# Cross attention of a streaming encoder layer: the samples' matmuls in column groups, splits cut by head and in quarters

## What is computed

```python
qx = (rms_norm(h, g_pre_x) @ wq_x).reshape(bsz, l, MEM_HEADS, MEM_HEAD_DIM)
s = jnp.einsum('bqhd,bmhd->bhqm', qx.astype(f32), mem_k.astype(f32)) / math.sqrt(MEM_HEAD_DIM)
p = jax.nn.softmax(s, axis=-1)
ox = jnp.einsum('bhqm,bmhd->bqhd', p, mem_v.astype(f32)).reshape(bsz, l, D_MODEL).astype(dtype)
h = h + rms_norm(ox @ wo_x, g_post_x)
```

## Time and profile before

| | before |
|---|---|
| median of 3 runs | 2054.76 us |
| profiled execution | 2048.69 us, span of its instructions 2046.7 us |
| PE busy | 1916.4 us, 94% of the span |
| DVE, ACT, POOL busy | 937.4, 540.9, 422.4 us |
| mean granted PE clock | 0.966 of 2.4 GHz |
| chain that ended last | PE 80%, DVE 11%, ACT 4%, issue 4% |

### The profile page before, as it was taken

How to read it: one execution, slowest core, us unless ns; L and a number is a source line. 1 busy time by engine, 2 the same in 40 slices (tenths; PEclk the granted TensorE clock), 3 DMA queues, 4 the chain that set the end, 5 groups by cost and what they waited for, 6 DMA issues and landing times.

```text
span 2046.7 us, 28884 instructions
## 1 busy us (share of the span) xinstructions
PE 1916.4 (94%) x12014; PEld 1850.7 (90%) x12014; DVE 937.4 (46%) x1600; ACT 540.9 (26%) x1144; POOL 422.4 (21%) x203
## 2 busy tenths in 40 slices
PE   7999989998777898989989899999999999999996
PEld 7998979998666798988889899999999999999995
DVE  6852276675775428324342752332232232333245
ACT  6432312224663325103232541001001001001023
POOL 0000001131000132310023233143153153153130
PEclk9999999998899899989989999999999999999998
DMA  5243122222105311122311221011011011011032
GB/s 192 73 146 130 57 90 84 62 83 86 32 11 173 110 42 41 62 101 106 129 57 42 94 72 49 24 52 52 21 52 52 21 52 52 21 62 42 21 113 93
DMA packets 61950, 146.22 MB, mean 71 GB/s; under 512 B 4352, under 2 KB 34432, under 8 KB 60288
## 3 DMA queue, kind: packets, MB, share of 16 engines
q1 hardware_dynamic: 33952, 103.53, 14.8%
q10 hardware_dynamic: 27872, 40.88, 5.8%
HBM read 120.95 MB, written 23.44 MB: 71 GB/s over the span
## 4 chain that ended last, share of the span: by engine, by line
PE 80%; DVE 11%; ACT 4%; issue 4%; DMA 1%; SPq 1%; ACTq 0%; DVEq 0%
PE bank L200 23%; PE bank L203 22%; PE bank L204 22%; PE bank L1088 2%; PE bank L1099 1%; PE bank L1058 1%; PE bank L887 1%; DVE NL L281 1%; PE bank L966 1%; PE bank L914 1%; DVE hid_l L2312 1%; DMA w_raw<-in_wall 1%; DVE at_sm L2043 1%; PE bank L267 1%; PE bank L736 1%
## 5 line engine op out<-in xcount | busy, mean ns | idle before, releaser
L203 PE MATMUL bank<-NL,w_hi 128*128 128x384 f32 x1800 | 609.0, 338 | 0.0
L200 PE MATMUL bank<-NH,w_hi 128*128 128x384 f32 x1608 | 548.7, 341 | 9.0 <-DVE NL L340 6.6
L204 PE MATMUL bank<-NH,w_lo 128*128 128x384 f32 x1608 | 543.8, 338 | 0.0
L581 POOL TENSOR_TENSOR w_hi<-w_raw,one 128x1024 fp32r<-128x1024 f32 x82 | 163.7, 1996 | 1006.8 <-PE bank L200 881.2
L203 PEld LDWEIGHTS bank<-NL,w_hi 128*128 128x128 f32 x1800 | 340.9, 189 | 2.3 <-issue 0.9
L200 PEld LDWEIGHTS bank<-NH,w_hi 128*128 128x128 f32 x1608 | 304.7, 189 | 11.4 <-DVE NL L340 6.7
L204 PEld LDWEIGHTS bank<-NH,w_lo 128*128 128x128 f32 x1608 | 304.4, 189 | 0.0
L583 POOL TENSOR_TENSOR w_lo<-w_raw,w_hi 128x1024 fp32r<-128x1024 f32 x90 | 232.0, 2579 | 104.9 <-ACT w_hi L332 98.4
L2295 DVE TENSOR_TENSOR ACC<-ACC,bank 128x384 f32<-128x384 f32 x240 | 132.2, 553 | 124.1 <-PE bank L204 124.0
L200 PE MATMUL bank<-hid_h,w_hi 128*128 128x384 f32 x528 | 181.8, 344 | 5.5 <-DVE ACC L2295 4.7
L203 PE MATMUL bank<-hid_l,w_hi 128*128 128x384 f32 x528 | 177.8, 337 | 0.0
(11 more groups left out here) (345 smaller groups left out, 2831.5 us busy)
## 6 DMA issues: line engine op xcount, KB each, us to landing
w_raw<-in_wall SPq DMA_DIRECT2D x130, 512.0 KB, 3.3
cK<-in_cmk SPq DMA_DIRECT2D x8, 1024.0 KB, 7.0
cV<-in_cmv SPq DMA_DIRECT2D x8, 1024.0 KB, 4.9
H<-in_xT SPq DMA_DIRECT2D x5, 1536.0 KB, 12.5
scratch_h<-H ACTq DMA_DIRECT2D x3, 1536.0 KB, 5.9
Hback<-scratch_h ACTq DMA_DIRECT2D x3, 1536.0 KB, 11.8
out_y<-Hback ACTq DMA_DIRECT2D x6, 768.0 KB, 3.6
Kb<-in_kc SPq DMA_DIRECT2D x6, 512.0 KB, 9.3
```

Of the source, the lines that this page charges most:

```text
L200: m = mm(out, ah, bh, start=(i == 0), stop=False)
L203: mm(out, ah, bl, start=False, stop=False)
L204: m = mm(out, al, bh, start=False, stop=(i == n - 1))
L581: pool.tensor_tensor(whi[s][:], raw[s % 2][:], bc(one[:, 0:1], [P, WI]), ALU.mult).then_inc(w_hi, 1)
```

## The change

1. **Column groups.** y_scores(b) becomes, for each half e of the head dimension, four matmuls with 32 columns of weights (16 queries and 16 zeros, xQz), each head writing its own 32 PSUM partitions. Scores then stand on 128 partitions instead of 64, and the vector and activation steps on them too. y_values(b) turns round: the probabilities are the weights (32 columns), the cached values move (256 columns), each head again on its own 32 partitions. Its output isn't transposed, so ACT copies it (`y_ocopy` to sO), PE transposes it (`y_otrans`, one round later) and DVE copies it to QX.
2. **First tile and keys by head.** QXh gets a place of its own, tile 0 gets its own QXl0, and ACT and DVE go head by head: query part, key part. The scores of a head wait for that head alone. QXl0 lies in the place of cK1, so SP waits for the scores of tile 0 before cK1.
3. **Quarters.** The first chunk's split behind either attention is made in four pieces of two k, high and low, and the first unit waits for each piece where it needs it.
4. The loads of q and k of a tile become two steps with a semaphore each; q's goes out a head earlier.
5. Some semaphores of the samples' self attention are used again (b_S, b_nb, b_exp, b_p) with counts that go on.

```diff
-                         [("xQbd", [P, 2, H * QB], F32), ("mkh", [P, KT, MEM], F32R), ("xE0", [P, H, MEM], F32), ("xE1", [P, H, MEM], F32),
-                          ("xPT", [P, 2 * H * P], F32), ("cK1", [P, KT, MEM], F32)],
+                         [("xQz", [P, 2, KT, 32], F32), ("mkh", [P, KT, MEM], F32R), ("xE0", [P, H, MEM], F32), ("xE1", [P, H, MEM], F32),
+                          ("xPT", [P, 2 * H * P], F32), ("QXh", [P, KT, P], F32R), ("cK1", [P, KT, MEM], F32)],
+                         [("under_cK1", [P, 8 * MEM + 2 * 256 + 3 * 1024 + KT * P], F32), ("QXl0", [P, KT, P], F32R)],
...
-                          ("cV0", [P, 2, D], F32), ("sE0", [64, MEM], F32), ("sE1", [64, MEM], F32),
-                          ("sPT", [P, 2, 64], F32)]))
+                          ("cV0", [P, 2, D], F32), ("sE0", [P, MEM], F32), ("sE1", [P, MEM], F32),
+                          ("sPT", [P, 2, P], F32), ("sO", [P, MEM], F32)]))
...
+                if split is not None and i % 2 == 0:
+                    nc.tensor.wait_ge(n_lo, split + i // 2 + 1)
...
+                if b == 1:
+                    sp.wait_ge(x_S, 1)
                 if b >= 2:
-                    sp.wait_ge(y_S, b - 1)
...
+                pe.wait_ge(ld_qk[w], 16 * max(2, t + 1))
...
+                if q in (4, 8):
+                    pe.wait_ge(n_lo, SPLIT_Y + q // 4 + 4)
+                lin_unit(pe, I_WO, 0, q, YH, NL, split=None if q else SPLIT_Y)
...
-            pe.wait_ge(mk_l, 1)
 
             def x_scores(t):
-                pe.wait_ge(x_ql, t + 1)
                 if t:
+                    pe.wait_ge(x_ql, t)
                     pe.wait_ge(x_exp, H * t)
                 for h in range(H):
+                    if t == 0:
+                        pe.wait_ge(mk_l, 2 * h + 2)
                     m = three(B[h // 2][:, MEM * (h % 2):MEM * (h % 2) + MEM],
-                              [(g("QXh")[:, k, :], g("QXl")[:, k, :], g("mkh")[:, k, :], g("mkl")[:, k, :])
+                              [(g("QXh")[:, k, :], g("QXl" if t else "QXl0")[:, k, :], g("mkh")[:, k, :], g("mkl")[:, k, :])
...
-                for k in range(KT):
-                    m = mm(B[6][0:64, 0:MEM], g("xQbd")[:, b % 2, 64 * k:64 * k + 64], g(f"cK{b % 2}")[:, k, :], start=(k == 0),
-                           stop=(k == KT - 1))
-                m.then_inc(y_S, 1)
+                    pe.wait_ge(b_exp, DB + b)
+                for e in range(2):
+                    for h in range(H):
+                        m = mm(B[6][rows_of(h), 0:MEM], g("xQz")[:, b % 2, 2 * h + e, :], g(f"cK{b % 2}")[:, 2 * h + e, :],
+                               start=(e == 0), stop=(e == 1))
+                m.then_inc(b_S, 1)
...
             def y_trans(b):
-                pe.wait_ge(y_p, b + 1)
+                pe.wait_ge(b_p, DB + b + 1)
                 if b:
                     pe.wait_ge(ys_o, b)
                 for k in range(2):
-                    m = nc.tensor.transpose(B[7][:, 64 * k:64 * k + 64], g(f"sE{b % 2}")[:, tok(k)], ident[0:64, 0:64])
...
             def y_values(b):
                 pe.wait_ge(y_Te, b + 1)
                 pe.wait_ge(ld_cv[b % 2], 16 * (b // 2 + 1))
-                for h in range(H):
-                    for e in range(2):
-                        o = B[7][:, P + DS * (2 * h + e):P + DS * (2 * h + e) + DS]
-                        for k in range(2):
-                            m = mm(o, g(f"cV{b % 2}")[:, k, tok(2 * h + e)], g("sPT")[:, k, DS * h:DS * h + DS],
-                                   start=(k == 0), stop=(k == 1))
+                for k in range(2):
+                    for h in range(H):
+                        m = mm(B[7][rows_of(h), MEM:2 * MEM], g("sPT")[:, k, rows_of(h)],
+                               g(f"cV{b % 2}")[:, k, MEM * h:MEM * h + MEM], start=(k == 0), stop=(k == 1))
                 m.then_inc(y_pv, 1)
+
+            def y_otrans(b):
+                pe.wait_ge(y_c, b + 1)
+                for e in range(2):
+                    m = nc.tensor.transpose(B[7][:, tok(e)], g("sO")[:, tok(e)], ident)
+                m.then_inc(y_ot, 1)
 
...
+                if i:
+                    y_otrans(i - 1)
                 x_trans(i)
                 if i + 1 < DB:
                     y_scores(i + 1)
                 y_trans(i)
                 x_values(i)
                 y_values(i)
+            y_otrans(DB - 1)
 
...
+            def load_qk(t, w):
                 if t > 2:
-                    act.wait_ge(a_tr, 2 * t)
+                    act.wait_ge(a_tr, 2 * t + w - 1)
                 dst = g("qkr" if t > 1 else f"qkp{t}")
-                s = ld_qk[1 if t == 1 else 0]
-                act.dma_start(dst[:, 0, :], q_d[P * t:P * t + P, :]).then_inc(s, 16)
-                act.dma_start(dst[:, 1, :], k_o[P * t:P * t + P, :]).then_inc(s, 16)
...
+            def split_high(c, dst, src):
+                for k in [slice(2 * i, 2 * i + 2) for i in range(4)] if c == 0 else [slice(0, KT)]:
+                    act_f(dst[:, k, cs(c)], src[:, k, cs(c)], ACT.Copy).then_inc(n_hi, 1)
+
             def y_high(c):
-                act_f(g("YH")[:, :, cs(c)], g("YT")[:, :, cs(c)], ACT.Copy).then_inc(n_hi, 1)
+                split_high(c, g("YH"), g("YT"))
...
-                act_f(g("sPT")[:].rearrange("p a n -> p (a n)"), B[7][:, 0:128], ACT.Copy).then_inc(y_Te, 1)
+                act_f(g("sPT")[:].rearrange("p a n -> p (a n)"), B[7][:, 0:MEM], ACT.Copy).then_inc(y_Te, 1)
+
+            def y_ocopy(b):
+                act.wait_ge(y_pv, b + 1)
+                if b:
+                    act.wait_ge(y_ot, b)
+                act_f(g("sO")[:], B[7][:, MEM:2 * MEM], ACT.Copy).then_inc(y_c, 1)
...
-                if t:
-                    act.wait_ge(x_S, t)
+                act.wait_ge(x_S, t)
                 act_f(g("QXh")[:], g("QX")[:, :, tok(t)], ACT.Copy).then_inc(x_qh, 1)
 
             act.wait_ge(lin_ev, 4 + 48)
             act.wait_ge(ld_mk, 16)
-            act_f(g("mkh")[:], g("mkT")[:], ACT.Copy).then_inc(mk_h, 1)
-            act.wait_ge(mk_l, 1)
-            q_high(0)
+            for h in range(H):
+                k = slice(2 * h, 2 * h + 2)
+                act_f(g("QXh")[:, k, :], g("QX")[:, k, tok(0)], ACT.Copy).then_inc(mk_h, 1)
+                act_f(g("mkh")[:, k, :], g("mkT")[:, k, :], ACT.Copy).then_inc(mk_h, 1)
...
+                y_ocopy(i)
             act.wait_ge(ys_o, DB)
             act.wait_ge(x_o, NT - 1)
             for c in range(CH):
-                act_f(NH[:, :, cs(c)], g("QX")[:, :, cs(c)], ACT.Copy).then_inc(n_hi, 1)
+                split_high(c, NH, g("QX"))
...
+            def split_low(c, base, src, hi):
+                for i in range(4 if c == 0 else 1):
+                    k = slice(0, KT) if c else slice(2 * i, 2 * i + 2)
+                    split_dve(dve, base + (3 + c if c else i), src[:, k, cs(c)], hi[:, k, cs(c)], NL[:, k, cs(c)])
+
             for c in range(CH):
-                split_dve(dve, SPLIT_Y + c, g("YT")[:, :, cs(c)], g("YH")[:, :, cs(c)], NL[:, :, cs(c)])
+                split_low(c, SPLIT_Y, g("YT"), g("YH"))
                 if c == 0:
                     o_scale(NT - 1)
...
-            link(nc.vector.memset(g("xQbd")[:], 0.0))
 
...
+                CP(g("xQz")[:, b % 2, :, 0:DS], QX[:, :, SEQ + DS * b:SEQ + DS * b + DS]).then_inc(y_q, 1)
+
+            for h in range(H):
+                k = slice(2 * h, 2 * h + 2)
+                dve.wait_ge(mk_h, 2 * h + 1)
+                TT(g("QXl0")[:, k, :], QX[:, k, tok(0)], g("QXh")[:, k, :].bitcast(F32), ALU.subtract).then_inc(mk_l, 1)
+                dve.wait_ge(mk_h, 2 * h + 2)
+                TT(g("mkl")[:, k, :], g("mkT")[:, k, :], g("mkh")[:, k, :].bitcast(F32), ALU.subtract).then_inc(mk_l, 1)
+            link(nc.vector.memset(g("xQz")[:], 0.0))
             y_lay(0)
             y_lay(1)
-            q_low(0)
 
             def x_max(t):
                 dve.wait_ge(x_S, t + 1)
...
             def y_out_(b):
-                dve.wait_ge(y_pv, b + 1)
-                CP(QX[:, :, SEQ + DS * b:SEQ + DS * b + DS], B[7][:, P:2 * P].rearrange("p (a q) -> p a q", a=KT)).then_inc(ys_o, 1)
+                dve.wait_ge(y_ot, b + 1)
+                CP(QX[:, :, SEQ + DS * b:SEQ + DS * b + DS].rearrange("p (h e) q -> p e h q", e=2),
+                   B[7][:, 0:MEM].rearrange("p (e h x) -> p e h x", e=2, h=H)[:, :, :, 0:DS]).then_inc(ys_o, 1)
...
+                    if i:
+                        y_out_(i - 1)
                     y_max(i + 1)
...
+                if i + 1 == DB:
+                    y_out_(i - 1)
                 x_out(i)
-                y_out_(i)
+            y_out_(DB - 1)
 
             for c in range(CH):
-                split_dve(dve, SPLIT_OX + c, QX[:, :, cs(c)], NH[:, :, cs(c)], NL[:, :, cs(c)])
+                split_low(c, SPLIT_OX, QX, NH)
             ACC = g("ACC")
```

(8 more changed lines are left out.)

69 lines of the change are left out of this document (29 added, 40 removed).

## The result

The changed kernel took 2023.85 us, the median of four runs (2017.43 to 2029.89), beside 2054.65 for the kernel before in the same comparison: a ratio of 0.984, with a 95% interval of 0.9812 to 0.9868. A second comparison gave 0.9851 (0.9824 to 0.9879), 2022.48 us. The forecast was 2035, the range began at 2022. So the direction was right, and the gain of some 31 us was 1.6 times the 19.4 of the sum. The profiled execution took 2017.43 us, its span 2015.4 against 2046.7.

The account below looks back on a forecast made before the run. PE was taken to bound the six rounds, the xPT chain just below. Gains 9.2 + 5.1 + 1.2 + 4.2 - 0.3 = 19.4 us gave 2029.3 profiled, 2035 as median; own range 2027 to 2041, with rivals 2022 to 2048.

Parts of the forecast that it names:

- v: y_scores and y_values: length of eight column-group matmuls, taken as 2.03 us between bounds of 0.90 and 3.60.
- the tail: Last round and tail: two shorter y_values gain 2.9 us, less 0.8 and 0.9 for added steps; gain 1.2.
- all four groups side by side: Rival for y_scores and y_values: v = 0.90 us, total 2026 us; chance 0.27.
- the drain: Objection: changing tiling mode drains the array; four steps a round at 0.12 us, 4 us in all, mostly inside the new wait.
- The new wait: Before x_values, for ACT's xPT: 1.2 us a round, absorbing y_scores' gain; round 13.39 us, six rounds gain 9.2.
- The half clock: Six rounds: the 6.3 us lost to PE's halved clock was left unchanged by the forecast.
- none or every round: Half clock in the rounds: none would give 6.3 us more, a half-clock stretch in every round 2 less.
- The start: Start of the attention, first tile by head: scores of tile 0 gain 5.6, tile 1 loses 0.5; gain 5.1 us.
- The projection: Output projection, split in quarters: wait from last copy to first matmul falls from 6.20 to 2.05 us; gain 4.2.
- the quarters behind the self attention: Behind the self attention the same split in four earns nothing, as PE waits for the scaling there; minus 0.3 us.
- the loads of q and k: Loads split into two steps: turn's wait ends behind ACT's o_evac, not a load; nothing taken, 0.5 us either side.
- The feared queue of loads behind cK1: Start: three loads queued ahead of cV1, held with cK1 until tile 0's scores end, could delay y_scores(1) 4 us.

Follow-up runs that it names:

- one_group: Changed kernel with all four heads' outputs written to the same 32 partitions, one column group: 3.57 us each for y_scores and y_values, 2029.42 us in one execution.
- neighbours_same_group: Changed kernel with the two matmuls of a head behind each other, so program neighbours share a column group: 1.02 us for the eight, 2020.36 us in one execution.
- changed_again: The changed kernel unaltered, run once more in a second comparison: 2022.48 us, ratio 0.9851 to the kernel before.
- xpt_halves: Changed kernel with x_values waiting for each half of xPT where it reads it: wait 1.67 us in six x_values, 2019.47 us in one execution.

## Why the prediction was off, step by step

**The step that failed** is the bound taken for v: "the two passes of one matmul use the same group, so they must follow each other, and if passes start in program order, only the second pass of one head overlaps the first of the next: 9 x 0.225 = 2.03". It put v 1.03 us too high; by the sum's own formula, one v in each of six rounds and two in the tail, that is 8.2 of the 11.9 us between the forecast gain and the measured 31.3. The premise about one group is right (one_group: 16 x 0.223), the one about the order is not (neighbours_same_group: 1.02 us even where neighbours share a group). The rival "all four groups side by side" with 0.90 us had the mechanism; 1.00 is measured, four bursts 0.22 apart and 0.1 more until the transposes start. The Trainium skill, "TensorE: Matmul & The Clock Gate", "Part 3: Packing small matmuls", whose three groups at 2.38 times had given an estimated 1.5 us, pointed to the right side; here four groups give 3.6. The start in program order, for which the prediction named it too, does not hold for the passes of these matmuls: 1.02 us is measured in neighbours_same_group, and that order would give 2.9. Of the drain that the Trainium skill, "TensorEngine Tiling (Array Packing)", "Key Properties", names for a change of mode, the trace leaves room for that 0.1 us and 0.1 more ahead of the groups: x_trans takes 0.96 before them and 0.87 in the last round, where y_trans follows at once. That the 0.1 is the drain is not shown.

**The new wait** was right in place and releaser, and too short because v was too long. Put 1.00 into the forecast's own formula: the round is 11.36 + 1.00 = 12.36, measured 12.41, and the wait 4.75 - 0.26 - 0.96 - 1.00 - 0.26 = 2.3, less the 0.2 by which y_trans' busy time of 0.44 runs past its 0.26; measured 2.06. With v = 1.00 the six rounds gain 15.3 and the tail 1.2 + 2.1 = 3.3, in all 27.6. The table reads 27.7, which is partly luck: 0.7 less in the rounds and 0.6 more at the start cancel. The other 3.6 us of the measured 31.3 are no term of the sum: 4.1 of less half clock and of pace behind the projection's start, less 0.5 for a later end of the query projection.

**The half clock** in the rounds was carried over at 6.3 us and came out at 81.22 - 6 x 12.41 = 6.8. The size held, the reason did not: it had sat in x_scores, behind y_values with 16 columns moving, and now sits in x_values, behind the wait. The prediction named both ways out, none or every round, and gave neither a mechanism. It should have asked what stands before each slow stretch: y_values with 16 columns moving, which the change removes. And a wait near's (2.03 us, followed by 0.50) was about to appear in every round.

**The start**: 5.1 forecast, 5.7 measured. The scores of tile 0 ran at full clock (3.63 us from first to last), which gave 6.75 in place of 5.6, and the scores of tile 1 behind the longer idle time cost 1.03 in place of 0.5. That the clock held is luck of this execution: in changed_again tile 0 took 4.69 us (909.60 to 914.29) and tile 1 4.72, a gain of 5.2 in all. **The projection** (4.2, 1.98 us behind the last copy; the later quarters, taken as 0.95 us each, are not always so quick, as shown above), the quarters behind the self attention and the loads of q and k (the turn's waits 10.9 us against 10.5 in all) came as said. The feared queue of loads behind cK1 did not appear: no wait of the PE in the rounds was released by a DMA.

What stays open: how passes are handed out among the groups; which length of idle time or which work before it decides the clock; and the paces of 0.1733, 0.1747 and 0.1766 us. On the clock the runs leave this: with waits of 2.04 to 2.07 us (1.95 to 2.28 in the first round) one to three of the six rounds stayed at full clock, with 1.67 all five, in one execution. But the first x_values was slow behind 1.89 us in xpt_halves and at full clock behind 1.95 in the changed kernel, and the one behind 0.91 above was slow from end to end. So the length of the wait alone does not tell.

## What to carry to other kernels

When work on the bounding engine shrinks, compute the next chain's length to the tenth of a microsecond and reorder it in the same change: here moving one copy ahead of four exponentials was worth 22 us on top of 30, and nothing without them. An idle time made in this way costs twice, once as the wait and once as half clock in the matmuls behind it, so a wait of 2.06 us in a round cost up to 2.06 + 1.62 = 3.7. Small outputs that stand on 32 partitions each are worth writing so, with the wide operand moving, in any order of the program: y_values went from 3.48 us to 1.00.

## What the runs showed of the hardware that I had not expected

Four column groups of fp32 matmuls, 256 columns moving, run 3.6 times as fast as one group (1.00 against 3.57 us for eight), whether neighbours in the program share a group or not. Matmuls with 16 columns moving keep the PE busy in the records (3.49 of 3.49 us) and are yet followed by half clock: 4.46 us for x_scores against 2.96. Behind an idle time of about 2 us in each round the next matmuls took 1.6 us more in three to five of six rounds; behind 1.67 us in none of five, in one execution. And a DVE subtraction of 0.95 us took 3.15 beside a POOL split of weights.
